# Moving the sampled tokens' cache attention of a hybrid decoder step from a stage of its own into the slots of the trunk

## The reference

```python
def gathered_window_attention(q, kbuf, vbuf, knew, vnew, window, dil, table, sink):
    kc = jnp.concatenate([kbuf, knew.astype(kbuf.dtype)], axis=1)
    vc = jnp.concatenate([vbuf, vnew.astype(vbuf.dtype)], axis=1)
    ...
    idx = lbuf + jnp.arange(T)[:, None] - steps[None, :] * dil
    kg = kc[:, idx].astype(jnp.float32)
    vg = vc[:, idx].astype(jnp.float32)
    ...
    logits = jnp.einsum('nthgd,ntshd->nthgs', qg, kg) + bias
    probs, lse = softmax_with_sink(logits, valid[None, :, None, None, :], sk)
    out = jnp.einsum('nthgs,ntshd->nthgd', probs, vg).reshape(n, T, H, dh)
```

## Time and profile before

| | us |
|---|---|
| median of 3 runs | 2942.93 (2936.24 to 2943.4) |
| profiled execution | 2942.64 |
| its span | 2940.5 |
| stage `attend_sample`, first DMA issue to that of `core` | 410.56 to 616.39 |
| block b = 1 from its first dense matmul | 1592 to 2072 |
| block b = 2 | 2076 to 2562 |
| block b = 3 | 2566 to 2940 |

### The profile page before, as it was taken

The page is one execution under the profiler, slowest core; times in us unless marked ns, Lnnn a source line. Parts: engine busy times, 40 slices in busy tenths (PEclk is TensorE's granted clock), DMA queues, the critical chain, the costliest instruction groups (busy, mean ns, idle before and its releaser), DMA issues.

```text
span 2940.5 us, 44206 instructions
## 1 busy us (share of the span) xinstructions
PE 2586.6 (88%) x18107; PEld 1571.5 (53%) x18107; DVE 1160.8 (39%) x2657; ACT 872.4 (30%) x1546; POOL 269.1 (9%) x304
## 2 busy tenths in 40 slices
PE   7799533659899779999998999899899989899999
PEld 4455413535455335555444655445465545688887
DVE  3345325325456526566422444520434431132222
ACT  3332104216564325434222432111432211211111
POOL 0011100012111012111001111000111100100000
PEclk9899655569999989999999999999999999999999
DMA  6334325254555464556673333443333344322222
GB/s 211 113 130 160 96 71 137 99 168 168 171 175 169 135 197 164 194 187 200 204 229 125 121 114 108 134 140 128 102 126 111 100 126 150 101 88 99 94 94 85
DMA packets 322671, 406.06 MB, mean 138 GB/s; under 512 B 62319, under 2 KB 254447, under 8 KB 320688
## 3 DMA queue, kind: packets, MB, share of 16 engines
q1 hardware_dynamic: 322480, 403.37, 43.0%
HBM read 296.08 MB, written 107.23 MB: 137 GB/s over the span
## 4 chain that ended last, share of the span: by engine, by line
PE 65%; DVE 5%; DMA 3%; ACT 3%; issue 2%; SPq 1%; POOL 0%; POOLq 0%; DVEq 0%; ACTq 0%
PE core_dense L2413 54%; PE core_spare L2530 2%; DMA core_js<-scratch_sums 2%; PE core_spare L2518 2%; PE core_spare L2506 1%; PE core_spare L2541 1%; PE core_dense L2438 1%; PE core_spare L2571 1%; DVE core_col L2283 1%; DVE core_h L2188 1%; PE core_spare L2593 1%; PE core_spare L2599 1%; DVE core_r L2165 0%; PE core_spare L2607 0%; DMA core_ring<-scratch_kept_w 0%
## 5 line engine op out<-in xcount | busy, mean ns | idle before, releaser
L2413 PE MATMUL core_dense<-core_u,core_ring 128*128 128x512 f16 (+2 forms) x4800 | 874.1, 342 | 17.7 <-DVE core_u L2161 17.5
L2413 PEld LDWEIGHTS core_dense<-core_u,core_ring 128*128 128x128 f16 x4800 | 470.9, 99 | 387.6 <-issue 32.3
L2413 PE MATMUL core_dense<-core_r_hi,core_ring 128*128 128x512 f16 (+2 forms) x2560 | 653.6, 341 | 2.5 <-DVE core_h L2188 2.5
L2413 PE MATMUL core_dense<-core_r_lo,core_ring 128*128 128x512 f16 (+2 forms) x1280 | 437.3, 342 | 0.0
L2413 PEld LDWEIGHTS core_dense<-core_r_hi,core_ring 128*128 128x128 f16 x2560 | 252.0, 98 | 201.2 <-issue 11.3
L2413 PE MATMUL core_dense<-core_pu,core_ring 128*128 128x512 f16 x1152 | 267.8, 390 | 25.6 <-DMA core_pu<-scratch_u 18.1
L2188 DVE SCALAR_TENSOR_TENSOR core_h<-core_dense,core_h 128x512 f32<-128x512 f32 (+2 forms) x160 | 94.4, 590 | 494.2 <-PE core_dense L2413 494.0
L2030 ACT ACTIVATE core_r<-core_dense 128x512 f32<-128x512 f32 (+2 forms) x160 | 82.6, 516 | 573.0 <-PE core_dense L2413 573.0
L2176 DVE TENSOR_TENSOR core_r<-core_r 128x512 f32<-128x512 f32 (+2 forms) x160 | 94.8, 592 | 360.5 <-ACT core_r L2030 360.5
L564 PE MATMUL tok_prod<-tok_w_hi,tok_u 128*128 128x512 f16 (+1 forms) x768 | 204.7, 356 | 0.0
L2413 PEld LDWEIGHTS core_dense<-core_pu,core_ring 128*128 128x128 f16 x1152 | 115.2, 100 | 158.8 <-issue 21.8
(11 more groups left out here) (340 smaller groups left out, 3108.3 us busy)
## 6 DMA issues: line engine op xcount, KB each, us to landing
core_ring<-scratch_kept_w SPq DMA_DIRECT2D x264, 512.0 KB, 3.7
scratch_kept_w<-core_ring SPq DMA_DIRECT2D x72, 512.0 KB, 5.3
core_qkv<-out_tok SPq DMA_DIRECT2D x48, 384.0 KB, 4.5
core_w_raw<-in_w_up SPq DMA_DIRECT2D x32, 512.0 KB, 4.6
core_w_raw<-in_w_down SPq DMA_DIRECT2D x32, 512.0 KB, 4.5
out_tok<-tok_tok SPq DMA_DIRECT2D x16, 644.0 KB, 3.0
smp_kc<-in_c_kt SPq DMA_DIRECT2D x8, 1152.0 KB, 8.1
smp_v<-in_c_v SPq DMA_DIRECT2D x8, 1152.0 KB, 5.0
```

The costliest lines, as they stand in the source:

```text
L2413: ins = pe.matmul(bank, w[:, k, part, :], s, start=first and j == 0, stop=last and j == 2, skip_group_check=True)
```

## The change

`attend_sample` is replaced by `settle`, an empty block in which GpSimd clears the semaphores. Its work becomes units of `core`:

```diff
+                    some += [[]] * (56 - len(some))
+                    if b == 1:
+                        some[1] = some[1] + [("sq", 0, 0, 0)]
+                        for k in range(16):
+                            some[4 + 3 * k] = some[4 + 3 * k] + [("sk", k // 2, k % 2, 0)]
+                    if b == 2:
+                        for k in range(3):
+                            some[2 * k] = some[2 * k] + [("sx", k, 0, 0)]
+                        for k in range(16):
+                            some[8 + 2 * k] = some[8 + 2 * k] + [("sv", k // 2, k % 2, 0)]
+                        some[41] = some[41] + [("se", 0, 0, 0)]
```

`sq` transposes the new queries and keys, `sk` scores sequence n for head pair j, `sx` is the softmax in three parts, `sv` multiplies with the values, `se` adds the new rows' share and makes the output's two fp16 parts. The banks that they claim:

```diff
+            elif kind == "sk":
+                for bank in (4, 5):
+                    claim(("SK", b, i), bank, smp_taken, 2 * b + i + 1)
+            elif kind == "sx" and b == 0:
+                for bank in (0, 1):
+                    claim(("SN",), bank, smp_step, SCORED)
+                claim(("SR",), 2, smp_step, SCORED)
+            elif kind == "sx" and b == 2:
+                claim(("SP",), 2, smp_copied, COPY_P)
+                claim(("SM",), 0, smp_copied, COPY_P)
+            elif kind == "sv":
+                claim(("SV", b, i), 5, smp_taken, 16 + 2 * b + i + 1)
```

Keys and values are no longer split; PE multiplies them in fp32. A head pair stands on two halves of the partitions, and its two halves write banks 5 and 4:

```diff
+                    elif kind == "sk":
+                        ...
+                        pe.wait_ge(piece_in[j], 16 * (4, 2)[j] * (n + 1))
+                        free(pe, "SK", n, j)
+                        if j == 0:
+                            for q in range(2):
+                                for s in range(2):
+                                    rows = slice(HD * s, HD * s + HD)
+                                    at = 12 + DEC_T * q
+                                    pe.matmul(spare[5 - s][:, at:at + DEC_T], piece[rows, j, KC * P:], qs[rows, q, DEC_T * n:DEC_T * n + DEC_T], start=True, stop=True)
+                        for k in range(KC):
+                            ...
+                            for s in range(2):
+                                rows = slice(HD * s, HD * s + HD)
+                                ...
+                                last = pe.matmul(spare[5 - s][:, at:at + w], piece[rows, j, k * P:(k + 1) * P], qs[rows, 2 + j, q0:q0 + w], start=True, stop=True)
+                        last.then_inc(smp_done, 1)
+                    elif kind == "sv":
+                        ...
+                        if j == 0:
+                            pe.matmul(bank[:, 8:24], piece[:, j, KC * P:], st[:, 0:4, DEC_T * n:DEC_T * n + DEC_T], start=True, stop=True)
+                        ...
+                        for k in range(KC):
+                            ...
+                            last = pe.matmul(out[:, :, t0:t0 + w], piece[:, j, k * P:(k + 1) * P], st[:, s0:s0 + 2, q0:q0 + w],
+                                             start=k == 0, stop=k == KC - 1, skip_group_check=True)
+                        last.then_inc(smp_done, 1)
```

DVE copies each result out of the banks (four or two copies) and signals `smp_taken`. SP loads the next piece of a pair when `sk` or `sv` of it is done, four DMAs for j = 0 and two for j = 1 in the first pass, two and one in the second; the pieces lie where block 0 had its raw weights (`piece`, which `w_raw` now shares). Behind `sk` (7, 0), in slot 46 of block 1, SP issues the biases:

```diff
+                def load_biases():
+                    sp.wait_ge(smp_done, 15)
+                    for kind in range(4):
+                        ...
+                        for hh in range(4):
+                            ...
+                            sp.dma_start(b_old[rows, kind, :], lines_at(io, kind, near + P - 1, [[0, DEC_N], [t_step, DEC_T], [1, P]])).then_inc(smp_in, 16)
+                            sp.dma_start(b_new[rows, kind, :], lines_at(io, kind, near + 2 * P - 1, [[0, DEC_N], [LINE - 1, DEC_T], [1, DEC_T]])).then_inc(smp_in, 16)
+                    sp.dma_start(masks, io["masks_s"]).then_inc(smp_in, 16)
```

More of the change, by code:

```diff
@@ L1148, in _ @@
+        a = Alloc(nc, ctx, "settle", before)
+        with nc.Block() as block:
             @block.gpsimd
@@ L1321, in core @@
         ring = a.sb("ring", [P, R, 8, 2, P], F16)
-        w_raw = a.sb("w_raw", [P, RW, 8, P])
+        piece = a.sb("piece", [P, RW, 10 * P])
+        w_raw = [piece[:, i, 0:8 * P].rearrange("p (k c) -> p k c", c=P) for i in range(RW)]
         x = a.sb("x", [P, XR, 5, P])
@@ L1368, in core @@
         rate = a.sb("rate", [P, HB])
-        dt_x = a.sb("dt_x", [P, NT, HB])
-        dt_e = a.sb("dt_e", [P, NT, HB])
-        dt_y = a.sb("dt_y", [P, NT, HB])
-        dt_l = a.sb("dt_l", [P, NT, HB])
+        dt_all = a.sb("dt_all", [P, 4, NT, HB])
+        dt_x, dt_e, dt_y, dt_l = (dt_all[:, i, :, :] for i in range(4))
         small = a.sb("small", [P, NT, 5, HB])
@@ L1814, in finish @@
                         load_sums(b + 1)
+                    elif kind == "sq":
+                        load_keys(0, 0)
+                        load_keys(0, 1)
+                    elif kind == "sk":
+                        if b + 1 < DEC_N:
+                            load_keys(b + 1, i)
+                        elif i == 0:
+                            load_biases()
+                    elif kind == "sx" and b:
+                        load_values(0, b - 1)
+                    elif kind == "sv" and b + 1 < DEC_N:
+                        load_values(b + 1, i)
+                    elif kind == "se":
+                        store_sampled()
                 y_taken = {}
@@ L1873, in _ @@
                             load_x(0, j)
+                    if kind == "up" and i == 0 and b == 1:
+                        load_stok()
                     if kind == "up" and i == 31 and b + 1 < NB:
@@ L1956, in split @@
                         act.wait_ge(raw_in[n % RW], 16 * (n // RW + 1))
[L1957 removed]
+                        act.activation(ring[:, q % R, :, 0, :], w_raw[n % RW], ACT.Copy, scale=WS).then_inc(hi_split, 1)
                 def take_col(n, i):
@@ L2647, in build @@
     last = None
-    for stage in (tokens, scan_sample, attend_sample, core):
+    for stage in (tokens, scan_sample, settle, core):
         last = stage(nc, io, last)
```

485 lines of the change are left out of this document (217 added, 268 removed).

## The result

The changed kernel takes **2873.1 us** (median of 4 runs, 2867.5 to 2873.7), the kernel before, run beside it, 2943.2. The ratio is 0.976, 95% interval [0.975, 0.977]: 2.4% faster, 8 us above the forecast of 2865. The profiled execution took 2873.65 us with a span of 2871.4, so 69.1 us of span are gone.

The account below looks back on a forecast made before the run. TensorE was taken to bound the trunk, with the removed stage as exposed time. -204.8 + 76.9 + 22.9 + 32 + 2 - 7.1 = -78.1 us on 2942.64 gave 2865 us, range 2830 to 2915.

Parts of the forecast that it names:

- What goes: The removed stage before the trunk, 410.56 to 616.39: -205.8 us, with 1 us for the added boundary -204.8.
- PE instructions: Small matmuls moved into the trunk: key units 37.8 us, values' units 35.4, the rest 3.7, together 76.9.
- Waits: TensorE waits at the moved units, mostly for banks: 22.9 us, 14.5 of it at key units; bounds 12 to 35.
- The clock: Half clock around moved units: five places at 3.4 us, five at 1.7, one in five of 20 at 1.7: 32 us.
- The burst: 33 bias load issues ahead of a weight fetch make it some 3 us late; 2 us taken, bounds 0 to 6.
- What is hidden: Units in slots 37, 38 and 40 cover TensorE's waits for the join: -7.1 us, bounds -11 to -2.
- Rival 1: Only waits pull the clock down, small matmuls do not: clock term 5 us instead of 32, 2838 us; chance 0.25.
- Rival 2: The key units' row halves do not pair: +36 us and some +9 of clock, 2910 us; chance 0.13.
- Rival 3: Slower than before, the clock staying down around every unit: 109 us instead of 32, plus 73, 3015 us; chance 0.03.
- rival 4: The removed time is not all given back: trunk's first load waits grow or `settle` costs more, at most +5 to 10 us.

Follow-up runs that it names:

- e3_unpaired: The changed kernel with each key unit doing all matmuls of the lower partition half, then all of the upper, instead of alternating: 2922.7 us.
- e2_wide_keys: The changed kernel with each key matmul moving 96 columns instead of 1 to 4, surplus results overwritten or never read: 2853.6 us.
- e5_front_wide: The changed kernel with units ahead in their slots, 96 columns per key matmul and each values' product computed 32 times side by side: 2829.4 us.
- e4_wide_values: The changed kernel with only the values' units' products computed 32 times side by side (64 columns in most blocks, 256 in each unit's first): 2869.3 us.
- e1_front: The changed kernel with each moved unit ahead of its slot's other work instead of behind it: 2845.1 us.
- e8_half_wide: Against the kernel with other slots (2808.7 us), the values' units' columns are repeated 16 times instead of 32: 2806.9 us.

## Why the prediction was right, step by step

- **What goes.** Forecast -204.8, measured -205.1 (first load of the trunk at 411.24 for 411.6).
- **PE instructions.** Forecast 76.9. At full clock the key units take 2.55 and 2.11 us (58 ns a record, forecast 56), together 37.3 for 37.8; the values' units 2.15 and 1.93, together 32.6 for 35.4; the rest some 3.8 for 3.7. In all 73.7: the pairing read from the earlier trace rows was right, and e3_unpaired shows it.
- **Waits.** Forecast 22.9, measured 21.6: 14.3 before the key units (3.07, 0.53, 2.73, 1.18, 0.75, 2.58, 3.25 and 0.25 in slots 4 to 31, each within 0.1 us of what the prediction read for that slot), 3.5 before the values' units, 3.8 at the softmax parts.
- **The clock: the mis-sized term.** Forecast 32, measured 43.2: 31.6 us in the dense line (21.2 + 10.4), 9.4 in the key units (46.7 us for 37.3) and 2.2 in the values' units (34.8 for 32.6). The records of the granted clock give the same sum: 60.6 and 25.8 us more at 0.50 in blocks 1 and 2, and half of 86.4 is 43.2. What failed is the count of the falls. Where a unit had no wait or a short one, I let one in five fall; of the nine key units without any wait or with the 0.25 us of slot 31, seven did. These seven hold 27.3 us at half clock, 6.8 of which the join had before; half of the rest is 10.2 us of time, where my price for nine such units is 3.1. The sites with waits came out nearly right: slots 4, 10, 19 and 25 hold 30.7 us at half clock, 15.4 us of time for 13.6, and slots 7, 13 and 16 hold 10.2, 5.1 us of time as forecast. That the unit itself runs at half clock, as in slot 10, is in these stretches already. The values' units fell less often (4 of 16), so block 2 came out nearly right (12.6 us against some 11) and block 1 too low (30.6 against some 22). The places that I counted, 5, 5 and 20, are also two short of 32 units, 0.7 us by my own price. The bounds of 5 and 45 held it.
- **The burst.** Forecast 2, measured 1.6, before slot 50:

```profile
1821.55 2.76 PE L2344 MATMUL core_dense<-core_u,core_ring 128*128 128x512 f16 x12 [1.60 <-DMA core_ring<-scratch_kept_w]
```

  The step's own words, less where the clock has fallen, hold. Between the burst's first issue and the end of the ring's stock, the kernels whose clock did not fall waited 3.13 us (e2_wide_keys) and 3.46 us (e5_front_wide), those with 3.4 us at 0.50 waited 1.60 (after) and 1.53 (e4_wide_values), and those with 6.8 and 7.7 us, e1_front and e3_unpaired, did not wait. Part of the burst's cost was hidden by slower dense work.
- **What is hidden.** Forecast -7.1, measured -6.7: the join waits fell from 9.3 to 5.2 us in block 1 and from 9.3 to 6.7 in block 2.

Measured terms: -205.1 + 73.7 + 21.6 + 43.2 + 1.6 - 6.7 = -71.7, to which block 0 adds 1.7 and some 0.9 us stay unaccounted for: -69.1. The forecast was -78.1; of the 9 us between them the clock has 11, and the cheaper instructions give 3 back.

**The rivals.** Rival 1 (only the waits pull the clock down) is out by e1_front and e2_wide_keys: with either cause alone 33 to 43 us of half clock are left in block 1, with both away 19. Its argument, that the slots of the earlier trace rows from 1606 to 1790 are one third small work and stayed at 1.00, overlooked that those matmuls have 65 or 128 moving columns, where the units have 1 to 16. Rival 2 is out in the changed kernel; built as e3_unpaired it costs 50 us, for 45 in its price (36 and 9). Rival 3 has its mechanism, with the clock down around 13 of 16 key units, but between units it always came back: half clock cost 43 us in both blocks, not the 109 behind the units and 73 in them that rival 3 needed. Of rival 4 nothing was seen but the 1.7 us of block 0.

The Trainium skill ("TensorE: Matmul & The Clock Gate", LDWEIGHTS) also says that the time of a weight load goes by columns, whatever the rows. The trace agrees for unpaired 64-row loads, 112 ns from start to start beside the earlier trace rows's 112 for 128 rows; that two 64-row loads in alternation take 58 each does not follow from it.

**Open.** Why the key units lose the clock two to three times as often as the values' units (13 and 14 of 16 in two kernels against 4 to 6 in three), at nearly the same length (2.11 to 2.55 us against 1.93 to 2.15), was not separated: they differ in length, in rows (64 against 128) and in what stands beside them.

## What to carry to other kernels

When small work moves from a stage of its own into a dense stream, add to its instructions and its waits a term for the clock, and count in it the small work itself: here 43 us beside 74 and 22. Matmuls whose pace is set by the weight load can move more columns at nearly no cost (up to 128 here), and that kept the clock up where one to four columns let it fall (4 of 16 key units against 13, with the waits as they were). Place such a unit ahead of work that has just been handed to another engine, not behind it: its banks are then free. Order alone was worth 28 us, most of it in block 1, where 14.3 us of waits stood before the units; with wide columns, the bias loads in parts and other slots it was 66. And read the price of a small matmul from the starts, not from the busy time of its group, which holds the latency.

## What the runs showed of the hardware

- The granted clock falls to 0.50 behind a 2.6 us group of one- and four-column fp32 matmuls with TensorE busy throughout (slot 22 of after), and does not behind the same weight loads with 96 columns (slot 22 of e2_wide_keys).
- Moving 96 columns instead of 1 to 4 made a group of 44 records 2.63 us long for 2.55 (e2_wide_keys). With fp32 weights of 128 rows, records of 2 to 128 columns follow each other after 110 to 113 ns at full clock (after, e4_wide_values, e8_half_wide), those of 256 after 216 to 220 ns (e4_wide_values).
- fp32 weight loads of 64 rows go at 58 ns a record if the two row halves alternate (after), at 112 within a half if they don't (e3_unpaired; 102 over the unit).
- A wait for DMA can be shorter because the clock is low. Before the same ring load TensorE waited 3.1 and 3.5 us with no time at half clock since the burst of issues (e2_wide_keys, e5_front_wide), 1.5 and 1.6 with 3.4 us of it (e4_wide_values, after), and not at all with 6.8 and 7.7 (e1_front, e3_unpaired).
